# Gated delta rule: the squares of queries and keys are summed as fp32r parts instead of in fp32

## What is computed

```python
def l2_norm(x):
    return x * lax.rsqrt(jnp.sum(x * x, -1, keepdims=True) + EPS)

def hybrid_mixer(h, w_in, dn_conv, ...):
    proj = h @ w_in
    (dn_q, dn_k, dn_v, dn_z, dn_a, dn_b, gl_q, gl_k, gl_v, gl_g, gl_r) = jnp.split(proj, offsets, axis=-1)
    qkv = jax.nn.silu(causal_dwconv(jnp.concatenate([dn_q, dn_k, dn_v], -1), dn_conv))
    q, k, v = (a.reshape(bsz, t, DN_HEADS, DN_HEAD_DIM) for a in jnp.split(qkv, 3, axis=-1))
    ...
    o_dn = gated_delta_rule(l2_norm(q), l2_norm(k), v, log_a, beta)
    ...
    o_gla = gla_attention(...)
```

## Time and profile before

| | |
|---|---|
| median of 3 runs | 3337.12 us (3335.78 to 3339.93) |
| profiled execution | 3342.04 us |
| its span, first to last instruction | 3340.3 us |
| mean granted TensorE clock | 0.995 |
| busy | TensorE 98%, VectorE 59%, ScalarE 39% |
| stage of the change (projections of the second block) | 2040 to 2410 us of the span |

### The profile page before, as it was taken

The page is one execution under the profiler, slowest core; times in us unless marked ns, Lnnn a source line. Parts: engine busy times, 40 slices in busy tenths (PEclk is TensorE's granted clock), DMA queues, the critical chain, the costliest instruction groups (busy, mean ns, idle before and its releaser), DMA issues.

```text
span 3340.3 us, 38691 instructions
## 1 busy us (share of the span) xinstructions
PE 3270.5 (98%) x15672; PEld 2679.9 (80%) x15672; DVE 1957.4 (59%) x2362; ACT 1319.3 (39%) x1888; POOL 462.2 (14%) x369
## 2 busy tenths in 40 slices
PE   8999999999999999999999999999999999999998
PEld 6888888887877788888888887777788778888886
DVE  8564462333756444687873275445476788888226
ACT  4342211444266523433331147353555554444213
POOL 0000000000000000444440020000020035554000
PEclk9999999999999999999999999999999999999999
DMA  3314242112511124233338323121204323324721
GB/s 125 78 57 136 89 168 66 52 51 77 184 64 32 57 89 137 77 114 114 107 119 329 126 85 115 63 95 44 101 1 171 114 89 114 111 106 173 295 97 51
DMA packets 116402, 356.91 MB, mean 107 GB/s; under 512 B 16232, under 2 KB 26216, under 8 KB 116208
## 3 DMA queue, kind: packets, MB, share of 16 engines
q1 hardware_dynamic: 114112, 354.10, 30.4%
q10 hardware_dynamic: 2112, 0.33, 0.1%
HBM read 267.63 MB, written 85.58 MB: 106 GB/s over the span
## 4 chain that ended last, share of the span: by engine, by line
PE 87%; DVE 6%; ACT 4%; issue 1%; DMA 1%; SPq 0%; ACTq 0%; DVEq 0%
PE PS L496 46%; PE PS L2517 22%; PE PS L479 8%; PE PS L1980 1%; PE PS L1633 1%; PE PS L514 1%; DVE wlo L441 1%; PE PS L1608 1%; DVE FT L3834 1%; ACT whi L436 1%; PE PS L3961 1%; PE PS L1621 0%; PE PS L3972 0%; PE PS L1271 0%; DMA slot<-hid 0%
## 5 line engine op out<-in xcount | busy, mean ns | idle before, releaser
L441 DVE TENSOR_TENSOR wlo<-raw,whi 128x1024 fp32r<-128x1024 f32 (+3 forms) x380 | 482.1, 1269 | 392.8 <-ACT whi L436 390.2
L436 ACT CAST whi<-raw 128x1024 fp32r<-128x1024 f32 (+3 forms) x380 | 359.1, 945 | 692.5 <-PE PS L496 340.8
L496 PE MATMUL PS<-xhi,whi 128*128 128x512 f32 x1872 | 602.1, 403 | 7.8 <-DVE wlo L441 2.6
L496 PE MATMUL PS<-xlo,whi 128*128 128x512 f32 x1872 | 579.3, 391 | 0.0
L496 PE MATMUL PS<-xhi,wlo 128*128 128x512 f32 x1872 | 578.2, 390 | 0.0
L496 PEld LDWEIGHTS PS<-xhi,whi 128*128 128x128 f32 x1872 | 345.3, 189 | 92.5 <-issue 15.3
L496 PEld LDWEIGHTS PS<-xlo,whi 128*128 128x128 f32 x1872 | 352.4, 188 | 75.6
L496 PEld LDWEIGHTS PS<-xhi,wlo 128*128 128x128 f32 x1872 | 352.2, 188 | 75.1
L2517 PE MATMUL PS<-tf,whi 128*128 128x512 f32 x936 | 288.1, 389 | 0.0
L2517 PE MATMUL PS<-xhi,whi 128*128 128x512 f32 x624 | 243.6, 390 | 2.5 <-DVE xlo L2502 2.5
L2517 PE MATMUL PS<-xlo,whi 128*128 128x512 f32 x624 | 243.3, 390 | 0.0
(11 more groups left out here) (613 smaller groups left out, 5484.4 us busy)
## 6 DMA issues: line engine op xcount, KB each, us to landing
raw<-in_w_up SPq DMA_DIRECT2D x88, 512.0 KB, 3.8
hid<-hs SPq DMA_DIRECT2D x88, 512.0 KB, 3.6
raw<-in_w_in SPq DMA_DIRECT2D x67, 512.0 KB, 3.5
slot<-hid SPq DMA_DIRECT2D x56, 512.0 KB, 7.0
adr<-in_w_ada SPq DMA_DIRECT2D x48, 512.0 KB, 4.8
raw<-in_w_down SPq DMA_DIRECT2D x40, 512.0 KB, 3.6
raw<-in_w_gate SPq DMA_DIRECT2D x32, 512.0 KB, 3.5
merged<-hid SPq DMA_DIRECT2D x16, 512.0 KB, 12.8
```

Of the source, the lines that this page charges most:

```text
L436: act.e.copy(whis[place(i)][:, ks, :], raws[i % RING][:, ks, :]).then_inc(*give("w_hi", i))
L441: dve.e.tensor_tensor(wlos[place(i)][:, ks, :], raws[i % RING][:, ks, :], whis[place(i)][:, ks, :].bitcast(F32), ALU.subtract).then_inc(*g ...
L496: ins = pe.e.matmul(ps[:, h * 512:(h + 1) * 512], w[s][:, k, :], x[:, h * 512:(h + 1) * 512], start=(at == 0 and n == 0), stop=(at == kt - ...
```

## The change

Ones are made twice at the start: the memset, then a copy onto itself that rounds to fp32r, and c_ones is given by the copy. The fp32 name `ones` is a view of the same bytes.

For each of the eight tiles of queries and keys, ScalarE rounds the squares (in `sq`) to fp32r and writes them over the tile's own `raw`, right behind the Square and after a wait for it. VectorE subtracts them from the squares, in place in `sq`. This stands directly behind the tile's own convolution in VectorE's order, ahead of the next slot, and waits for ScalarE's step. TensorE sums both parts with the fp32r ones: four matmuls of 128x512 in place of two fp32 ones. It waits for the low part instead of the squares. `raw` of queries and keys is freed by the sum, not by the convolution. No transfer and no other work is added or moved.

```diff
-        ones = mem("ones", base + 2752, [128, 128])
+        ones_r = mem("ones", base + 2752, [128, 128], F32R)
+        ones = ones_r.bitcast(F32)
...
-            dve.e.memset(ones, 1.0).then_inc(*give("c_ones"))
+            dve.e.memset(ones, 1.0).then_inc(*dve.step())
+            dve.wait_ge(*dve.last)
+            dve.e.tensor_copy(ones_r, ones).then_inc(*give("c_ones"))
...
+        wkr = [tile("wkr", wk_at + n * TB, F32R) for n in range(4)]
...
-                WK_USES += [("raw", ft, ("conv", ft)), ("sq", ft, ("unit", ft))]
+                WK_USES += [("raw", ft, ("unit_ss", ft)), ("sq", ft, ("unit", ft))]
...
+        def work_part(kind, ft):
+            return wkr[WK_AT[kind, ft] % 4]
...
                 ps = psum.take(pe, dense, f"u{ft}", ("unit_root_ln", ft))
-                pe.wait_ge("unit_sq", ft)
-                sum_over_partitions(pe, ps, work_tile("sq", ft), True, True, "unit_ss", ft)
+                pe.wait_ge("unit_lo", ft)
+                for h in range(2):
+                    for part in ("raw", "sq"):
+                        ins = pe.e.matmul(ps[:, half[h]], ones_r, work_part(part, ft)[:, half[h]], start=(part == "raw"), stop=(part == "sq"))
+                ins.then_inc(*give("unit_ss", ft))
...
                 act.e.activation(work_tile("sq", ft), proj_dst(ft), ACT.Square).then_inc(*give("unit_sq", ft))
+                act.wait_ge("unit_sq", ft)
+                hi_of(act, work_part("raw", ft), work_tile("sq", ft), "unit_hi", ft)
...
+            def unit_low(ft):
+                lo = work_part("sq", ft)
+                dve.wait_ge("unit_hi", ft)
+                lo_of(dve, lo, work_tile("sq", ft), work_part("raw", ft), "unit_lo", ft)
+
...
                     conv(ft)
+                    if kind != "v":
+                        unit_low(ft)
                     later.append((lambda ft=ft: token(ft)) if kind == "v" else (lambda ft=ft: unit(ft)))
```

## The result

| | before | after |
|---|---|---|
| median | 3337.55 us (6 runs, 3335.76 to 3339.93) | 3350.20 us (6 runs, 3346.50 to 3353.02) |
| profiled span | 3340.3 us | 3348.8 us |
| mean granted clock | 0.995 | 0.993 |

The change makes the kernel slower, by 12.7 us between the medians; the ratio is 1.0034, 95% interval 1.0024 to 1.0044. The forecast was 3348.7 us, range 3341 to 3354.

The account below looks back on a forecast made before the run. TensorE, busy 98%, was taken as the bound, with ScalarE's and VectorE's chains ending almost with it. Schedule +7.1 us and clock +4.5 us sum to +11.6 us on the median 3337.12: 3348.7 us, range 3341 to 3354.

Parts of the forecast that it names:

- The sums: On TensorE, each sum over partitions of a q or k tile falls from 1.72 to 0.91 us, 6.5 us over eight.
- The added steps: Per q or k tile, a cast on ScalarE of 1.04 us and a subtraction on VectorE of 1.22 us.
- The schedule: TensorE's later work around the k sums of blocks 0 to 3 (k0 to k3): +1.26, +2.6, +1.26, +1.95, together +7.1 us.
- k1's wait: TensorE waits some 4.3 us for the low part before the sum of block 1's keys, making it 2.6 us later.
- the 2.4 and 3 us for gat and the root: TensorE's waits: 2.4 us twice for masked scores (gat), 3 us for the other group's root before the product of z.
- some 13: Sign of the forecast: all of TensorE's waits together grow by some 13 us; otherwise it is wrong.
- The clock: TensorE's granted clock falls after k0, k1, k2 and k3, 1.5 us each, k3's costing 0: +4.5 us.
- The rival by the Trainium skill: Only one long unbroken wait makes the clock fall, at k1 and perhaps k3: +8.6 us, 3345.7 us; chance 0.17.
- in time: Rival: the low part is ready when TensorE's sums need it, the gain stays: -6.5 us, 3330.6 us; chance 0.08.
- only part of the delay: Rival: part of the delay gets through, as where a ScalarE copy catches up: +3 to +6, 3341.6 us; chance 0.07.
- no fall: Rival: TensorE's clock does not fall behind the waits, leaving the schedule alone: +7.1 us, 3344.2 us; chance 0.10.
- the fp32 rate: Rival: fp32r sums on TensorE run at 0.86 us a matmul, 20 us more, 3365 us and above; chance 0.02.

Follow-up runs that it names:

- e1: The changed kernel plus 46 fp32r matmuls with overwritten results, issued by TensorE ahead of the sums of k0 to k3: 3346.33 us, ratio 1.0022 to the kernel before.
- e7: The changed kernel with the masked scores moved ahead of the weights' low part on VectorE in slots 7 and 21: 3346.95 us, ratio 1.0026 to the kernel before.
- e10: The changed kernel with masked scores ahead of the weights' low part and the second GLA pair's root behind q3's Exp: 3340.80 us, ratio 1.0006 to before.
- e11: As e10, but masked scores stand between the convolution of k0 (k2) and its low part: 3338.31 us, ratio 0.9999 to the kernel before.
- e9: The kernel before, fp32 sums kept, with masked scores ahead of the weights' low part and the second root behind q3's Exp: 3334.70 us, ratio 0.9987.
- e4: Against the changed kernel, Square writes fp32r itself, no cast or low part, sums of two fp32r matmuls: 3341.13 us, ratio 1.0010 to the kernel before.
- e12: As e11, plus 18 fp32r matmuls with overwritten results ahead of the sum of k1: 3336.09 us, ratio 0.9995 to the kernel before.
- e3: The changed kernel with its added steps and waits kept, but TensorE sums the squares in fp32 as before: 3349.39 us, ratio 1.0028 to the kernel before.

## Why the prediction was right

- **The sums**, 0.81 us less each: held. q1's sum in the changed kernel takes 0.93 from start to start (2189.31 to 2190.24), before 1.72: 0.79 less.
- **The added steps**, 1.04 and 1.22 us: 1.05 and 1.23. The cast of ones took 0.23 us (0.17 forecast); VectorE sat idle 2.00 us behind it and TensorE's first matmul came no later (4.83 us, before 5.28), so its 0 held too.
- **The schedule**, +1.26, +2.6, +1.26, +1.95 in the four blocks: e1 shows +1.28, +2.61, +1.29, +1.95. Every step of it held, k1's wait (4.3 forecast, 4.54 measured; the prediction's own starts, 2205.6 against 2202.20 less 0.30 and 0.81, give 4.5) and the 2.4 and 3 us for gat and the root (2.14 and 2.94) among them. TensorE's waits in the stage grew by 11.4 us, from 9.9 to 21.3; I had said some 13. The three kinds that I named grew by 12.8, and the wait of 1.4 for v3's SiLU went, covered by the slower product.
- **The clock**: right that it falls, too small in size. A fall was forecast at each of the four, and came at each. But the price of one was taken as 1.5 us. At k0 and k2 it is 1.6; at k1 it is 2.60, with a clock of 0.57 over 8 us instead of 0.60 over 4; at k3, put at 0 as covered by the wait for v3's SiLU, it is 1.20, because the wait of 1.4 us covers only part of a fall that loses about 2.6. The clock's share in this trace is 7.0 us, not 4.5; this term of the sum was mis-sized. It also differs from trace to trace: behind the same wait of 4.54 us at k1 the part is +5.08 to +5.34 in three kernels (the changed one, e7, e10) and +4.19 in e11, so one fall there costs 1.6 to 2.7 us. By the medians of the changed kernel and e1 the share is about 5.2 us, an estimate, nearer to my 4.5. My upper bound of 1.7 for one fall was read off 4 us after the startup and was too low. The trace of the kernel before had a longer one, outside the stage, that I did not look at:

```profile
728.00:736.00 8.00, 7.38 (x27) 6.45 (x28) 1.55 (x2) 1.41 (x2) 0.00 (x0) 0.58 0.21 70
```

  8 us at 0.58 lose up to 3.4 us.
- **The whole**: +12.7 us between medians against +11.6. The stage alone is +14.1 in the profiled execution, whose span is only 8.5 us longer. By the granted clock outside the stage, that execution loses about 6 us less there than the one of before (an estimate; one fall behind the stage instead of two, and none near 800 and 2720 us). That the forecast came within 1.1 us of the medians is partly luck: the clock's term was too small for this trace, and the mean price of a fall was not measured.
- **The range.** The forecast's own, 3345 to 3353, does not come out of the bounds named for it: a schedule of 7.1 give or take 1.5 and three falls of 0 to 1.7 give 3342.7 to 3350.8. The measured median lies in both.
- **The rival by the Trainium skill** (TensorE: Matmul & The Clock Gate, section HAM oscillation) would have had falls at k1 and perhaps k3 only. The falls at k0 and k2, behind waits of 1.12 and 2.14 us with a sum between them, decide against it; the granted clock over the next 4 us at k0 was 0.60.
- The rivals "in time" and "only part of the delay" fell with the waits of the earlier trace rows grown as forecast, "no fall" with the granted clocks behind them, and "the fp32 rate" with k3's sum, whose four records take 1.17 us.

## What to carry to other kernels

A busy share of 98% does not say that cutting TensorE's work shortens anything: look at which wait ends last behind the piece that is cut, and price the chain up to it. Where an added step feeds TensorE, count all that is queued behind it on its engine and behind whoever waits for it; here two steps of another strand were late only by their place in a queue, and moving them was worth more (e9) than the cheaper instruction without the moves (e4). A new wait of TensorE costs itself and can cost the clock behind it, so a saving that turns into waiting can end up as a loss, as in e4.

## What the runs showed of the hardware

- Less work made the kernel slower: in e4 TensorE waited 3.1 us at k0, and its granted clock over the next 7 us was 0.53 on average, where the kernel before waited 0.6 us and kept 1.00.
- Matmuls whose result nobody reads, issued into a wait, kept the granted clock at 1.00 and made the stage 7.0 us shorter in one kernel (e1) and 1.6 us in another (e12), by one trace each.
- Two shorter waits near each other can be followed by a fall: at k0 of the changed kernel, waits of 1.12 and 2.14 us with a sum between them were, with a granted clock of 0.60 over the next 4 us. With 1.12 and 1.00 us (e7), and with 0.31 and 1.35 us (e3), there was none.
- The length of a fall is not fixed by the wait before it: behind 4.54 us of wait the granted clock averaged 0.57 over 8 us in the changed kernel and 0.79 in e11.
- ScalarE's Square writes fp32r directly in the same time as fp32: 1060 and 1061 ns for 128x1024, by the rows of e4 and of before. So the rounded squares need no rounding step of their own. The low part needs the unrounded squares as well, and no run tries both parts in this way.
